# One matrix unit of three moved out of the mix loop into the recurrence's inversion steps, with its weights split by GpSimd

## The reference, cut to what matters

```python
xr, xw, xk, xv, xa, xg = (h + xx * mu[j] for j in range(6))
r, k, v, g = xr @ w_in[0], xk @ w_in[1], xv @ w_in[2], xg @ w_in[3]
decay = exp(-exp(w_log(xw)));  a = sigmoid(a0 + (xa @ a1) @ a2)
kk = normalised(k * k_k);      k = k * (1 + (a - 1) * k_a)
# for each head, step by step over the tokens
S = S * w_t - (S kk_t)(a_t kk_t)^T + v_t k_t^T;   y_t = S r_t
y = group_norm(y);  bonus = sum(r * k * r_k) * v
out = ((y + bonus) * silu(g)) @ w_out
```

## Time and profile before

| | us |
|---|---|
| median of 3 runs (2111.18 to 2115.22) | 2113.08 |
| the profiled execution | 2113.75 |
| its span in the trace | 2112.0 |
| gate units and preparation | to 137 |
| mix loop, 16 tiles | 137 to 432 |
| recurrence, 9 turns | 430 to 868 |
| PE busy over the span | 2013.4 (95%) |
| DVE, ACT, POOL busy | 1418.9, 1008.1, 174.7 |

### The profile page before, as it was taken

How to read it: one execution, slowest core, us unless ns; L and a number is a source line. 1 busy time by engine, 2 the same in 40 slices (tenths; PEclk the granted TensorE clock), 3 DMA queues, 4 the chain that set the end, 5 groups by cost and what they waited for, 6 DMA issues and landing times.

```text
span 2112.0 us, 42671 instructions
## 1 busy us (share of the span) xinstructions
PE 2013.4 (95%) x16558; PEld 1629.3 (77%) x16558; DVE 1418.9 (67%) x2272; ACT 1008.1 (48%) x1765; POOL 174.7 (8%) x183
## 2 busy tenths in 40 slices
PE   5999999988888889999999999999999999999998
PEld 4877777777777776788888888888667778888886
DVE  7788888876666664555563655799786776445355
ACT  6666666645656665333232332442665434334243
POOL 5230000000233332200000000000000000000000
PEclk9999999999999999999999999999999999999999
DMA  4445555563333322233333333333113322333332
GB/s 121 122 143 164 168 178 183 178 139 74 94 74 75 89 59 82 80 90 99 99 96 98 95 99 90 100 90 100 50 41 100 100 70 81 99 95 95 100 92 78
DMA packets 395952, 215.19 MB, mean 102 GB/s; under 512 B 85136, under 2 KB 374312, under 8 KB 395816
## 3 DMA queue, kind: packets, MB, share of 16 engines
q1 hardware_dynamic: 395608, 213.18, 35.2%
q10 hardware_dynamic: 208, 0.06, 0.0%
HBM read 181.68 MB, written 31.52 MB: 101 GB/s over the span
## 4 chain that ended last, share of the span: by engine, by line
PE 86%; DVE 6%; ACT 3%; issue 3%; DMA 1%; SPq 1%; POOL 0%; DVEq 0%; ACTq 0%; POOLq 0%
PE bank L1911 23%; PE bank L1913 23%; PE bank L1912 23%; PE bank L596 3%; PE bank L573 1%; PE bank L604 1%; PE bank L506 1%; PE bank L547 1%; PE bank L520 1%; PE bank L1108 1%; PE bank L526 1%; ACT inv L821 1%; PE bank L539 1%; DVE inv L922 1%; PE bank L553 1%
## 5 line engine op out<-in xcount | busy, mean ns | idle before, releaser
L1911 PE MATMUL bank<-xl,w_hi 128*128 128x512 f32 x1568 | 615.7, 393 | 3.9 <-DVE xl L2633 2.5
L1912 PE MATMUL bank<-xl,w_lo 128*128 128x512 f32 x1568 | 611.1, 390 | 0.0
L1913 PE MATMUL bank<-xl,w_hi 128*128 128x512 f32 x1568 | 611.0, 390 | 0.0
L1558 ACT ACTIVATE w_hi<-w_raw 128x1024 fp32r<-128x1024 f32 x278 | 293.1, 1054 | 481.9 <-PE bank L1913 477.4
L2202 DVE TENSOR_TENSOR w_lo<-w_raw,w_hi 128x1024 fp32r<-128x1024 f32 x278 | 342.6, 1232 | 48.7 <-ACT w_hi L1558 40.0
L1911 PEld LDWEIGHTS bank<-xl,w_hi 128*128 128x128 f32 x1568 | 294.5, 188 | 76.6 <-issue 9.9
L1913 PEld LDWEIGHTS bank<-xl,w_hi 128*128 128x128 f32 x1568 | 294.8, 188 | 61.9
L1912 PEld LDWEIGHTS bank<-xl,w_lo 128*128 128x128 f32 x1568 | 294.9, 188 | 60.6 <-issue 0.5
L1911 PE MATMUL bank<-xh,w_hi 128*128 128x512 f32 x448 | 183.0, 409 | 10.9 <-DVE xh L2207 10.7
L1913 PE MATMUL bank<-xh,w_hi 128*128 128x512 f32 x448 | 175.5, 392 | 0.0
L1912 PE MATMUL bank<-xh,w_lo 128*128 128x512 f32 x448 | 175.4, 392 | 0.0
(11 more groups left out here) (385 smaller groups left out, 3165.5 us busy)
## 6 DMA issues: line engine op xcount, KB each, us to landing
w_raw<-in_a_w_in SPq DMA_DIRECT2D x64, 512.0 KB, 4.2
w_raw<-in_b_w_in SPq DMA_DIRECT2D x64, 512.0 KB, 4.1
w_raw<-in_w_ffn_up SPq DMA_DIRECT2D x42, 512.0 KB, 4.0
w_raw<-in_w_in SPq DMA_DIRECT2D x36, 512.0 KB, 3.8
w_raw<-in_a_w_out SPq DMA_DIRECT2D x16, 512.0 KB, 4.2
w_raw<-in_b_w_out SPq DMA_DIRECT2D x16, 512.0 KB, 4.0
w_raw<-in_w_ffn_down SPq DMA_DIRECT2D x16, 512.0 KB, 4.1
d_g<-sq SPq DMA_DIRECT2D x16, 256.0 KB, 2.2
```

What stands on the lines that cost most here:

```text
L1558: A(w_hi[0:rows, slot, 0:nkb, 0:ncol], w_raw[0:rows, slot, 0:nkb, 0:ncol], ACT.Copy).then_inc(s_hi, units)
L1911: mm(outp, wh, xlo, start=start, stop=False)
L1912: mm(outp, wl, xhi, start=False, stop=False)
L1913: return mm(outp, wh, xhi, start=False, stop=stop)
```

## The change

The v unit leaves the mix tile. The values of pair 0 (two units) run behind the mix loop; those of pairs 1 to 7 run inside turns 0 to 6 of the recurrence, for the pair after, each unit as 8 blocks of three matmuls: unit a=0 at steps 9 to 15, unit a=1 at steps 16 to 22, one block a step and two at steps 15 and 22, all in PSUM bank 4. ScalarE copies the results out (`value_out`, at steps 16 and 23), and SP stores them for the bonus. GpSimd rounds and subtracts the weights of all value units but the first three and those of the first two output units (`value_weights`). The bonus is no longer multiplied by v in the mix tile: ScalarE copies its head sum (`bonus_copy`), and GpSimd multiplies it in `finish`, one more instruction for each of the 16 tiles. The bonus matmuls of tile j stand in tile j+1. SP's `mix_tile` has one panel and one store fewer, and the store of o_bv comes a tile later. The buffers ra and bt change places with Y, and since xl[2] (the v input) must stay in place during the recurrence, the first ten tiles of Y (Y_STAGED = 5 pairs) go to memory and come back in turn 7.

```diff
+        Y_STAGED = 5
+        VALUE_BLOCKS = {s: [(0, s - 9)] for s in range(9, 15)}
+        VALUE_BLOCKS[15] = [(0, 6), (0, 7)]
+        VALUE_BLOCKS.update({s: [(1, s - 16)] for s in range(16, 22)})
+        VALUE_BLOCKS[22] = [(1, 6), (1, 7)]
...
                     if when(t - 1, PAIRS):
                         chain(t - 1, s // 3, s % 3)
+                    if t + 1 < PAIRS:
+                        for a, k in VALUE_BLOCKS.get(s, ()):
+                            if (a, k) == (0, 0):
+                                if t == 0:
+                                    pe.wait_ge(s_n2m, CI)
+                                if t >= 2:
+                                    pe.wait_ge(R["y_rstd_made"], 2 * t - 2)
+                            if (a, k) == (1, 0):
+                                pe.wait_ge(s_free[0], values_read(t + 1))
+                            value_part(t + 1, a, k)
...
+            def value_out(t, a):
+
+                act.wait_ge(s_unit, U_VAL + 2 * (t + 1) + a + 1)
+                act.wait_ge(s_vspill[a], 16 * (t + 2))
+                copy_values(a, bank[4])
...
                 gp.wait_ge(R["ends_loaded"], LOAD_ENDS * (q + 1))
+                o(G.tensor_tensor(st_bv[a][:], st_bv[a][:], st_bonus[a][:], ALU.mult))
...
+            def value_weights(n):
+
+                gp.wait_ge(s_raw[n % 2], panels_by(n))
+                gp.wait_ge(s_unit, n - 1)
+                G.tensor_copy(w_hi[:, n % 2], w_raw[:, n % 2]).then_inc(s_hi, 1)
+                gp.wait_ge(s_hi, n + 1)
+                G.tensor_tensor(w_lo[:, n % 2], w_raw[:, n % 2], w_hi[:, n % 2].bitcast(F32), ALU.subtract).then_inc(s_lo, 1)
...
                     finish(t - 2, 1)
+                if when(t, PAIRS):
+                    value_weights(U_VAL + 2 * t + 3)
+                if when(t, PAIRS - 1):
+                    value_weights(U_VAL + 2 * t + 4)
...
                 mix_lora(*then)
                 mix(*then, 0)
                 mix(*then, 1)
+                if not first:
+                    spill_bonus(2 * t + a - 1)
                 spill_rates(t, a)
-                mix(*then, 2)
                 spill_rest(t, a)
...
-            panel(U_OUT1, 0, i["a_w_out"][0], 0, KB, 0)
-
+            for a in range(2):
+                value_panel(U_VAL + a)
+            spill_bonus(CI - 2)
...
             sp.wait_ge(s_spill, SPILL_MIX + SPILL_TILE * (CI - 1))
...
             load_q(0, 0)
             load_keys(0)
-            sp.wait_ge(s_unit, U_MIX + 3 * (CI - 1) + 2)
-            load_values(0)
+            value_panel(U_VAL + 2)
             load_q(0, 1)
             spill_rates(CI // 2 - 1, 1)
             spill_rest(CI // 2 - 1, 1)
+            sp.wait_ge(s_unit, U_VAL)
+            load_decays(0)
...
+                if t == PAIRS - 1:
+                    sp.wait_ge(s_yspill, 16 * (2 * Y_STAGED + 1))
+                    sp.wait_ge(s_unit, U_OUT1)
+                    sp.dma_start(Y[:, 0:2 * Y_STAGED, :],
+                                 d_y[0:2 * Y_STAGED].rearrange("k p t -> p k t")).then_inc(s_yback, 16)
...
-                w_high(n0 + 1, 1 - a, panels(U_MIX, 6, t, 3 * a + 1))
-                w_high(n0 + 2, a, panels(U_MIX, 6, t, 3 * a + 2))
+            def bonus_copy(j):
+                act.wait_ge(s_bon, j + 1)
+                A(o_bv[:], bank[5][:], ACT.Copy).then_inc(s_bonus, 1)
...
                 A(sum_hi[:], kk[:], ACT.Square).then_inc(s_sqhi, 1)
+                if not first:
+                    bonus_copy(j - 1)
+                w_high(n0 + 2, 0, panels(U_MIX, 4, t, 2 * a + 2))
                 act.wait_ge(s_zw, j + 1)
                 sigmoid(zw[:]).then_inc(s_sw, 1)
...
-                w_high(n0 + 3, 1 - a, panels(U_MIX, 6, t, 3 * a + 3))
+                w_high(n0 + 3, 1, panels(U_MIX, 4, t, 2 * a + 3))
...
+            def copy_values(a, summed):
+                A(st_v[:, a, 0:T], summed[:], ACT.Copy)
+                A(st_v[:, a, T:T + C], summed[:, 0:C], ACT.Copy).then_inc(s_free[a], 1)
...
+            def value_part(p, a, k):
+
+                n = U_VAL + 2 * p + a
+                if k == 0:
+                    pe.wait_ge(s_lo, n + 1)
+                last = three(bank[4][:], w_hi[:, a, k, :], w_lo[:, a, k, :], xl[2][:, 0, k, :], xl[2][:, 1, k, :],
+                             k == 0, k == KB - 1)
```

More of the change, by code:

```diff
@@ L226, in program @@
         n2, sqk, kraw = over("n2", [P, T]), over("sqk", [P, T]), over("kraw", [P, T])
-        o_r, o_v, o_bv = over("o_r", [P, T]), over("o_v", [P, T]), over("o_bv", [P, T])
+        o_r, o_bv = over("o_r", [P, T]), over("o_bv", [P, T])
         o_q, o_pc = over("o_q", [P, T]), over("o_pc", [P, NCH])
@@ L248, in program @@
         head_mean = over("head_mean", [P, P])
+        st_bonus1 = over("st_bonus1", [P, T])
         assert spot <= xh_at
         spot = xh_at
-        Y = over("Y", [P, CI, T])
+        ra, bt = [], []
+        for n in range(2):
+            ra.append(over(f"ra{n}", [P, 2, NCH, 2, C]))
+            bt.append(over(f"bt{n}", [P, 2, NCH, P]))
         assert spot == big_at
-        x_back, _, _ = place("x_back", [P, NT, D], F32, big_at + 2 * 32768)
+        x_back, _, _ = place("x_back", [P, NT, D], F32, xh_at)
         st_q = [over(f"st_q{n}", [P, 2, NCH, 3, C]) for n in range(2)]
@@ L847, in recurrence_scalar @@
                         y_out(q, 1)
+                    if s == 16 and when(t, PAIRS - 1):
+                        value_out(t, 0)
                     if s == 12 and when(t - 1, PAIRS):
@@ L2017, in _, with bonus @@
             repeat(pe, CI // 2 - LORA_TURNS, gate_turn)
+            def bonus(j):
+                pe.wait_ge(s_rklo, j + 1)
+                mm(bank[5][:], ones_r[:], sum_lo[:], start=True, stop=False)
+                mm(bank[5][:], ones_r[:], sum_hi[:], start=False, stop=True).then_inc(s_bon, 1)
             def mix(t, a):
-                j, n0 = 2 * t + a, 6 * t + (U_MIX + 3 * a)
-                free = [3 * t + (FREE_MIX + (3 * a + u) // 2) for u in range(3)]
-                unit(n0, a, xl[0], free=free[0])
+                j, n0, free = 2 * t + a, 4 * t + (U_MIX + 2 * a), 2 * t + (U_MIX // 2 + a)
+                first = isinstance(j, int) and j < 1
+                unit(n0, 0, xl[0], free=free)
+                if not first:
+                    bonus(j - 1)
                 pe.wait_ge(s_w2lo, j + 1)
-                if isinstance(j, int) and j < 1:
+                if first:
                     pe.wait_ge(s_lt, 1)
@@ L2033, in mix @@
                 last.then_inc(s_lunit, 1)
-                unit(n0 + 1, 1 - a, xl[1], free=free[1])
-                if isinstance(j, int) and j < 1:
+                unit(n0 + 1, 1, xl[1], free=free)
+                if first:
                     pe.wait_ge(s_ones, 1)
-                    pe.wait_ge(s_xlo, X_Y)
                 pe.wait_ge(s_sqlo, j + 1)
@@ L2041, in mix @@
                 mm(bank[4][:], ones_r[:], sum_hi[:], start=False, stop=True).then_inc(s_n2, 1)
-                unit(n0 + 2, a, xl[2], free=free[2])
-                pe.wait_ge(s_rklo, j + 1)
-                mm(bank[5][:], ones_r[:], sum_lo[:], start=True, stop=False)
-                mm(bank[5][:], ones_r[:], sum_hi[:], start=False, stop=True).then_inc(s_bon, 1)
             pe.wait_ge(s_xlo, X_Y - 1)
@@ L2054, in _ @@
             repeat(pe, CI // 2 - 1, mix_turn)
+            pe.wait_ge(s_xlo, X_Y)
+            unit(U_VAL, 0, xl[2], free=U_VAL // 2)
+            bonus(CI - 1)
+            unit(U_VAL + 1, 1, xl[2], free=U_VAL // 2)
             def out_part(n, k):
```

174 lines of the change are left out of this document (107 added, 67 removed).

## The result

The changed kernel takes 2219.72 us (median of 4 runs, 2216.09 to 2223.5) against 2112.13 us before (4 runs): a ratio of 1.051, 95% interval 1.0485 to 1.0535. The forecast was 2222.0. The profiled execution took 2223.5 us, the slowest of the four and 3.8 us above their median, so one stretch of it can be a few us longer than usual.

What follows compares the result with a forecast made beforehand. PE, without idle time in the mix loop, was taken to set the mix tile. 2113.75 + 21.7 (mix tile) + 9.7 (step to the recurrence) + 76.8 (turns) = 2222.0 us; own range 2185 to 2262, wider range 2160 to 2262.

Steps and rivals of the forecast that it cites:

- The mix tile: Mix loop: k panel queued behind o_c's store delays the sigmoid; a tile takes 20.05 us, not 18.5, +21.7 us in all.
- PE's clock: Mix loop: even at half clock, a unit taking 10.9 us instead of 5.5, the tile stays at 20.05 us.
- the 7 that the prediction names as a sign: Mix loop: PE idles about 7 us in every tile, to be seen in the profile after.
- The step: Last tile's kk to turn 0's first transposes: decays load behind the last stores, 25.8 us against 16.2, +9.7 us.
- The blocks: Turns 0 to 6: a turn with a chain grows by 11.4 us, turn 0 by 8.4, together +76.8 us.
- I take 4.0 of them as filled: Inversion part of a turn: blocks fill 4.0 us of PE's some 5 us of issue stops.
- The wait at step 16: In a turn, the second unit's first block waits for ScalarE to read bank 4: +1.6 us.
- Turn 0: First recurrence turn: no chain, more free time and no norm, so 8.4 us longer.
- GpSimd: Value weights in a turn: rounding 2.5 to 5.0 us, subtraction 2.5, hidden behind steps 9 to 15, nothing added.
- rival D: Turns: GpSimd is late with 5.0 us roundings, PE waits at step 16, 1.5 us a turn; 2232 us, chance 0.09.
- Turn 7: Spill and reload of Y beside turn 7, with idle queues: nothing, from 0 to 3 us.
- Rival C: Turns and mix loop: blocks cost bare pace, 0.68 us each, +31.5; mix tile 14.7 us, -53; 2102 us, chance 0.04.

Runs made afterwards that it cites:

- e1: Changed kernel with the k panel issued ahead of the three stores that wait for o_c, and SP's mix loop written out: 2153.8 us, ratio 1.0197.
- e2: Changed kernel with the load of pair 0's decays moved on SP's queue to right behind the load of its keys: 2215.33 us, ratio 1.0484.
- e3: Changed kernel with the second value unit's first block moved from step 16 to step 17: 2209.56 us, ratio 1.0451.
- e4: Changed kernel with the reload of Y cut into five 512 KB transfers, four of them waiting on the chain: 2218.95 us, ratio 1.0509.
- e7: Changed kernel with the reload of Y in five 512 KB transfers, each issued only when the one before has landed: 2216.62 us, ratio 1.0506.
- e6: Changed kernel with the recurrence's value weights rounded by ScalarE and subtracted by VectorE in place of GpSimd: 2224.39 us, ratio 1.0536.

## Why the prediction was right, point by point

**The mix tile: right.** +21.4 measured, +21.7 forecast. The order of events was as read: store at T, panel at T + 2.05 to 2.55, landing at T + 6.4 to 6.7, sigmoid at T + 7.3 to 7.7. e1 shows that the panel is the cause and not only there at the same time. The rest of the tile did take 12.6 us. The first tile was not quite unchanged, 19.7 us against 20.7; the fourteen others took 20.1 against 18.5, which is +22.4.

**PE's clock: right that it sets nothing.** The average in the mix loop fell to 0.85 of full speed, from 1.00, and no wait of VectorE for PE appeared in the loop. PE was idle for 4.7 us a tile, not for the 7 that the prediction names as a sign: it was busy for 15.4 us and not 13.0, since a part of the work ran at half clock.

**The step: right in kind, 2 us short.** +11.7 against +9.7. The store of the bonus landed 1.1 us later than put, and one of the keys' issues took 1.8 us, not 0.6. That a second wait, for the values, ended 3.8 us before, with ScalarE's rounding of the third value panel in front of it, was not seen. e2 found it.

**The blocks: the right mechanism, each term a little off.** Per turn with a chain, forecast 14.0 - 4.5 + 1.9 = 11.4, measured 13.3 - 5.2 + 1.7 = 9.8 (turns 1 to 6). The term "I take 4.0 of them as filled" was too small: all of the stops vanished, and they were 4.6 a turn (27.4 over 6); PE's other idle time shrank by 0.6, with 0.5 forecast. The blocks' own time was 0.7 us, 5%, lower. The wait at step 16 was 1.68 us, 1.6 forecast, and e3 gave 10 to 12 us back for seven of them. Turn 0 was 10.6 us longer, 8.4 forecast, but that is one profile: e4 and e7, which change nothing before turn 7, have it at 48.2 and 47.0 us, 7.3 and 6.1 more than before, with a granted clock of 0.94 and 0.97 where the changed kernel's profile has 0.92. Together 69.3 against 76.8. By the Trainium skill's page "Runtime: NRT & Kernel Launch", as I had read its section "Instruction fetch mechanics", the stops would have been something else and have stayed (+28 us); they went, against the waits after, and in the kernel before they end behind a packet of instructions.

The range has a slip in it: its upper end of 2262 goes with turns at +111, and with the +100 that is stated it would be 2251. The measured time lies inside either.

**GpSimd: right that it is hidden, wrong bounds.** 3.4 us for a set, below my 5.0 to 7.5. The lower bound, two two-operand instructions, was no bound for a one-operand copy of 1024 elements in 1.04 us. The block at step 16 waited only for ScalarE, never for the weights, and e6 shows the hiding; so rival D is out too.

**Turn 7: wrong.** "Nothing, from 0 to 3" for the reload of Y; it was 5.4 us in that turn, and some 7.6 from its first transposes to the end. The step that failed is "with idle queues": the queues were idle of other data, but PE's own instructions come by DMA as well, and I had supposed just that when I costed the blocks. The stops that it made are 4.15 and 2.07 us, and the clock that fell behind them took 1.5 us more. The errors of -7.5 and +7.6 cancelled in the total; without that luck the forecast would have been 8 us off.

**Rival C** (the blocks swallowed, at a bare pace) had it right that the idle time fills, and still a turn costs 9.8 us, over the 6.2 from which it decides; the panel alone decided the mix loop.

## What to carry to other kernels

Moving work off the bounding engine in one stage is worth what the next chain in that stage allows, so follow each panel from its place in the issuing queue to the instruction that needs it: here a rounding moved 12 us forward in ScalarE's order found its panel queued behind a store. Work put into an engine's idle time costs its own duration less what that idle time was: 7.0 us of idle in a turn of 49 took in 3.5 net of 13.3, and the engine was still the bound. Before using a third engine as a helper, look at what the others do beside it, and place it where they read PSUM. And a large transfer is not free because its own queue is idle: a stream of short matmuls needs its instructions by DMA at the same time.

## What the runs showed of the hardware

- While GpSimd ran a 2.4 us subtraction between SBUF buffers, VectorE's kp (0.54 us alone) took 2.69 and ended 0.28 us behind it; sum_lo (0.68 alone) took 1.45; operations from PSUM kept their 0.74 us.
- PE's stops for "issue" in runs of short matmuls are waits for its instructions: 33 of 34 in the recurrence before the change ended 1.2 to 1.8 us behind a 16 KB packet of an instruction queue. In the turns they vanished when three long matmuls stood between the short ones. In turn 7, with a DMA share of 1.00, a packet started only 1.86 us after PE had run out, and the stop was 4.15 us long. The section "Instruction fetch mechanics" of "Runtime: NRT & Kernel Launch" in the Trainium skill calls the crossing from one block of instructions to the next mostly hidden; in these runs it is so only with long matmuls in between.
- Such a stop can cost more than it lasts: the granted clock was 0.58 in the 4 us behind the stop of 4.15 us.
- GpSimd rounds 128x1024 from f32 in 1.04 us and subtracts in 2.35, where four copies of 128x256 at 1.26 each had suggested 5.
